# First conditioning of a hybrid decoder step: the rests all on VectorE, eight weight slots whole in fp32, the first norm's tiles made between the groups, the constants loaded in two parts

## The chip, the cores and the metric

The kernel runs on one core of one Trainium2 chip. The metric is the device time of one execution in microseconds, the median of several runs. The engines are TensorE (PE in the profile), VectorE (DVE), ScalarE (ACT), GpSimd (POOL) and SyncE (SP), which issues most of the transfers.

## What is computed

One step of a single-layer hybrid decoder, for a prompt of 256 tokens and a sample group of 8 sequences with 4 tokens each: 288 token columns in all. D_MODEL is 2048. The part that matters here is the start of the layer:

```python
ada = jnp.dot(jax.nn.silu(c), p["w_ada"]) + p["b_ada"]
sh1, sc1, gt1, sh2, sc2, gt2 = jnp.split(ada[:, None, :], 6, axis=-1)
h = _rmsnorm(x, p["g_norm1"]) * (1.0 + sc1) + sh1
(qkv_raw, z, a_raw, b_raw, dq, dk, dv, iq, ik, iw, gate_gdn, gate_dsa) = _split_cols(jnp.dot(h, p["w_in"]))
```

c has nine rows (one for the prompt, eight for the samples). Behind it come gated DeltaNet, sparse attention, their merge, a convolutional feed-forward part and a last norm; the other four parts of ada are made later in the kernel, among other work. All is fp32 outside.

## The kernel before

**Split products.** A product of fp32 accuracy is made of cheaper ones. A weight slot is a tile of 128 x (4 x 256) fp32, 512 KB. ScalarE rounds it into w_hi (function hi, L703, type fp32r); VectorE or GpSimd subtracts, rest = raw - w_hi (L1199 and L648), into the place where the raw values are; TensorE multiplies with both. For the conditioning (cond_slot, L1988 and L1992) the activations cact (silu(c), high part and rest, 20 columns) are the stationary side: four products of 256 columns with w_hi and four with rest. For w_in (slot, L2022, L2023 and L2027) the weights are stationary and h_hi and h_lo, 288 columns, run through: 16 products with w_hi, 8 with rest.

**First conditioning ("ada1").** 16 groups of four slots: group g makes 256 columns of shift1 (g < 8) or scale1 (g >= 8). A group sums into one bank; VectorE copies it (cond_copy, L1184) to cond_t, TensorE turns it with two small products against the constant fold (turn, L2010) and VectorE adds the bias (cond_bias, L1190) into ada. The even slots' rests are GpSimd's, the odd ones' VectorE's. In each group TensorE also multiplies one tile of squares of x by ones (norm_part, L2055), behind one ScalarE square (squares_of, L716). These loops are rolled, two groups per pass.

**First norm.** When all groups are done: rms on ScalarE (Ln and Exp, L722 and L724), then scale_shift on VectorE: amul = (1 + scale) * g (L1219), the samples' tile hs in three operations (L1224 to L1228), and for each of 16 tiles of x a product into hf (L1231); ScalarE adds the shift and rounds (h_round, L729 to L734), GpSimd makes h_lo (h_rest, L653), VectorE that of the samples (L1234). w_in's first product waits for hs_lo and for the h_lo of the first four tiles.

**Order.** Each engine runs its own list in the order written. SyncE loads the slots in order (L563, L568); a load waits for raw_free of its ring place, which TensorE gives when the slot is used. Rings: 8 raw tiles and 4 w_hi tiles in the conditioning, 6 and 3 in w_in. c, all constants, vec, heads_v and x are loaded from ScalarE's queue at the start. ScalarE's list has the square between the third and the fourth hi of each group; before the first it waits for x.

## Time and profile before

| | us |
|---|---|
| median of 3 runs (lowest, highest) | 2187.02 (2181.03, 2190.06) |
| profiled execution, whole | 2179.57 |
| its span in the profile | 2177.6 |
| TensorE busy | 2043.4 (94%) |
| VectorE, ScalarE, GpSimd busy | 802.3, 1024.2, 1458.8 |
| mean granted TensorE clock | 0.979 |

All times within the execution count from the span's start. "Busy" is the time in which an engine executes; the rest is waiting. The conditioning and the first norm take the first 148 us of the span.

### The profile page before, as it was taken

The numbers are of one execution on the slowest core, as the hardware profiler recorded it, in microseconds if no ns is written. First come the engines' busy times: TensorE is split into PE (matmuls) and PEld (weight loads), VectorE is DVE, ScalarE is ACT, GpSimd is POOL, SyncE is SP. The second block draws the span as 40 slices with busy tenths as digits, with TensorE's granted clock in tenths as the row PEclk, the third lists the DMA queues.
The fourth block names the chain that finished last, engine by engine and source line by source line (L and its number), as shares of the span: only waits on it lengthen the run. The fifth ranks groups of instructions, "written<-read, shape, count | busy, mean of one in ns | idle before, by whom it ended". The sixth has DMA issues, their size and how long they took to land.

```text
span 2177.6 us, 39902 instructions
## 1 busy us (share of the span) xinstructions
PE 2043.4 (94%) x15252; PEld 1953.2 (90%) x15252; DVE 802.3 (37%) x1833; ACT 1024.2 (47%) x1580; POOL 1458.8 (67%) x625
## 2 busy tenths in 40 slices
PE   5769999999899998999989969999999999999996
PEld 3559989999898897988989969999999999999996
DVE  4654644443534446354534122232112232113212
ACT  5564335664445445455453336555334444344432
POOL 5777555674665565656678658777777777777762
PEclk9989999999999999999999989999999999999998
DMA  9856533443566575565676434444454444455541
GB/s 341 287 169 205 174 116 132 146 158 126 178 213 210 198 244 194 201 227 199 238 220 216 140 113 143 167 164 164 165 166 168 167 164 164 164 166 169 167 166 68
DMA packets 128418, 390.76 MB, mean 179 GB/s; under 512 B 27490, under 2 KB 36002, under 8 KB 127778
## 3 DMA queue, kind: packets, MB, share of 16 engines
q1 hardware_dynamic: 107008, 365.74, 49.6%
q10 hardware_dynamic: 21282, 23.25, 3.3%
q8 instruction: 88, 1.44, 0.3%
q14 instruction: 40, 0.33, 0.1%
HBM read 379.99 MB, written 8.88 MB: 179 GB/s over the span
## 4 chain that ended last, share of the span: by engine, by line
PE 85%; DVE 5%; ACT 3%; issue 2%; POOL 2%; DMA 2%; DVEq 1%; ACTq 0%
PE bank L2022 23%; PE bank L2023 23%; PE bank L2027 23%; PE bank L1992 3%; PE bank L1988 2%; POOL rest_a L648 1%; DVE rest_a L1199 1%; PE bank L2369 1%; PE bank L2361 1%; DVE rest_b L1199 1%; PE bank L2372 1%; PE bank L2055 1%; DMA x<-in_x 1%; PE bank L2465 1%; PE bank L2292 1%
## 5 line engine op out<-in xcount | busy, mean ns | idle before, releaser
L648 POOL TENSOR_TENSOR rest_a<-raw_a,hi_a 128x1024 fp32r<-128x1024 f32 x217 | 536.4, 2477 | 267.3 <-ACT hi_a L703 266.9
L2022 PE MATMUL bank<-h_hi,hi_a 128*128 128x288 f32 x1592 | 439.9, 302 | 18.3 <-POOL h_lo L653 13.2
L2023 PE MATMUL bank<-h_lo,hi_a 128*128 128x288 f32 x1592 | 432.8, 297 | 0.0
L703 ACT ACTIVATE hi_a<-raw_a 128x1024 fp32r<-128x1024 f32 x257 | 270.7, 1058 | 339.3 <-PE bank L2027 267.0
L648 POOL TENSOR_TENSOR rest_a<-raw_a,hi_b 128x1024 fp32r<-128x1024 f32 x100 | 241.6, 2416 | 130.6 <-ACT hi_b L703 130.6
L2022 PEld LDWEIGHTS bank<-h_hi,hi_a 128*128 128x128 f32 x1592 | 303.0, 190 | 22.1 <-issue 19.6
L2023 PEld LDWEIGHTS bank<-h_lo,hi_a 128*128 128x128 f32 x1592 | 303.6, 191 | 0.4
L648 POOL TENSOR_TENSOR rest_b<-raw_b,hi_a 128x1024 fp32r<-128x1024 f32 x82 | 205.1, 2501 | 85.8 <-ACT hi_a L703 85.8
L2027 PE MATMUL bank<-h_hi,rest_a 128*128 128x288 f32 x1656 | 252.7, 295 | 0.5
L2027 PEld LDWEIGHTS bank<-h_hi,rest_a 128*128 128x128 f32 x1656 | 230.5, 188 | 1.9 <-POOL rest_a L648 1.9
L2022 PE MATMUL bank<-h_hi,hi_b 128*128 128x288 f32 x776 | 213.5, 301 | 0.5 <-ACT hi_b L703 0.5
L2023 PE MATMUL bank<-h_lo,hi_b 128*128 128x288 f32 x776 | 210.0, 296 | 0.0
L703 ACT ACTIVATE hi_b<-raw_a 128x1024 fp32r<-128x1024 f32 x119 | 125.9, 1058 | 144.1 <-PE bank L2027 110.8
L703 ACT ACTIVATE hi_a<-raw_b 128x1024 fp32r<-128x1024 f32 x98 | 103.7, 1058 | 140.1 <-PE bank L2027 109.7
L2022 PEld LDWEIGHTS bank<-h_hi,hi_b 128*128 128x128 f32 x776 | 146.8, 189 | 2.2 <-ACT hi_b L703 0.7
L2023 PEld LDWEIGHTS bank<-h_lo,hi_b 128*128 128x128 f32 x776 | 147.2, 190 | 0.3
L1863 DVE SCALAR_TENSOR_TENSOR x<-bank,ada,x 128x256 f32<-128x256 f32 x64 | 28.0, 479 | 321.0 <-PE bank L2027 321.0
L648 POOL TENSOR_TENSOR rest_c<-raw_c,hi_b 128x1024 fp32r<-128x1024 f32 x47 | 112.9, 2403 | 39.7 <-ACT hi_b L703 39.7
L648 POOL TENSOR_TENSOR rest_a<-raw_a,hi_c 128x1024 fp32r<-128x1024 f32 x39 | 93.8, 2405 | 56.1 <-ACT hi_c L703 56.1
L648 POOL TENSOR_TENSOR rest_b<-raw_b,hi_c 128x1024 fp32r<-128x1024 f32 x39 | 93.7, 2402 | 34.8 <-ACT hi_c L703 34.8
L648 POOL TENSOR_TENSOR rest_c<-raw_c,hi_a 128x1024 fp32r<-128x1024 f32 x39 | 94.0, 2409 | 31.3 <-ACT hi_a L703 31.3
L2022 PE MATMUL bank<-h_hi,hi_c 128*128 128x288 f32 x352 | 95.9, 298 | 17.0 <-ACT hf L734 17.0
(475 smaller groups left out, 4452.7 us busy)
## 6 DMA issues: line engine op xcount, KB each, us to landing
raw_a<-in_stream SPq DMA_DIRECT2D x423, 512.0 KB, 3.4
raw_b<-in_stream SPq DMA_DIRECT2D x167, 512.0 KB, 3.3
raw_c<-in_stream SPq DMA_DIRECT2D x94, 512.0 KB, 3.3
st<-in_state ACTq DMA_DIRECT2D x16, 512.0 KB, 5.4
out_state_s<-st ACTq DMA_DIRECT2D x8, 512.0 KB, 4.8
x<-in_x ACTq DMA_DIRECT2D x1, 2304.0 KB, 17.1
x<-in_x ACTq DMA_DIRECT2D x2, 1152.0 KB, 6.1
...
```

The lines of the kernel that those rows point to most:

```text
L648: nc.gpsimd.tensor_tensor(rest[r], raw[r], w_hi[q].bitcast(f32), ALU.subtract).then_inc(lo_ready, 1)
L703: A_(w_hi[q], raw[r], ACT.Copy).then_inc(hi_ready, 1)
L1199: T_(rest[r], raw[r], w_hi[q].bitcast(f32), ALU.subtract).then_inc(lo_dve, 1)
L1863: STT(xt[:, 0:SEQ], bank[2 * bs + c][:, 0:SEQ], gt[:, 0:1], xt[:, 0:SEQ], ALU.mult, ALU.add)
L1988: MM(out[0:2 * NCP, 0:CT * P], cact[:, s_ * KS + k, :, :].rearrange("p m n -> p (m n)"), w_hi[q][:, k, :], start=(s_ == 0 and k == 0), sto ...
L1992: last = MM(out[0:NCP, 0:CT * P], cact[:, s_ * KS + k, 0, :], rest[r][:, k, :], start=False, stop=(s_ * KS + k == KT - 1))
L2022: MM(banks[c][:, 0:N], w_, hi_of(k), start=(first and k == 0), stop=False)
L2023: ins = MM(banks[c][:, 0:N], w_, lo_of(k), start=False, stop=False)
L2027: ins = MM(banks[c][:, 0:N], rest[r][:, k, c * P:(c + 1) * P], hi_of(k), start=False, stop=(last_ and k == KS - 1))
L2055: MM(bank[7][:, 0:N], ones, sq[:, s_ % 2, :], start=(s_ == 0), stop=(s_ == KT - 1)).then_inc(sq_used, 1)
L2292: last = MM(bank[7][:, TURN_COL + c * NCP:TURN_COL + (c + 1) * NCP], cond_t[:, c * P:(c + 1) * P], cv["fold"][0:2 * NCP, :], start=True, s ...
L2361: ins = MM(blk(3, ch), bt[:, l % 2, ch, :], tt[:, 4 + ch, :], start=True, stop=True)
```

## The change

- **Order of the groups.** ADA_GROUP: shift and scale groups by turns, so that after each pair two tiles of h can be made. All loops of the stage are written out.
- **Rests.** All 56 rests of split slots are VectorE's (ada_rest). GpSimd has none in this stage; its list goes on with w_in's.
- **Whole slots.** Slots 1 and 3 of groups 8 to 11 are multiplied in plain fp32 (whole_slot: the unsplit c_f, ten columns, against the raw tile): no hi, no rest.
- **Squares.** Four ScalarE squares of four tiles each (square_quad, groups 2 to 5) into sq1; the 16 products with ones in groups 3 to 6, one behind each slot; rms behind group 7's hi.
- **x scaled in place.** VectorE multiplies x by the norm's factor, four tiles at a time (scale_x, groups 8 to 11). ScalarE makes h_hi and hf of two tiles from it (round_pair, from group 9 on), VectorE h_lo (lo_pair), and the samples' part four tiles at a time (samples, round_samples, lo_samples).
- **The end.** The last turn stands behind w_in's slot 0, the last pair is made while w_in runs.
- **Loads.** The constants are reordered; the first 268 columns are loaded at the start, the other part by SyncE behind w_in's sixth load; w_in's slot 1 waits for it. x is loaded from ScalarE's queue behind the third hi.

```diff
+WHOLE = [4 * n + s for n in range(8, 12) for s in (1, 3)]
+SPLIT_BEFORE = [j - sum(1 for w in WHOLE if w < j) for j in range(2 * KT // CT * (KT // KS) + 1)]
+NSPLIT = SPLIT_BEFORE[-1]
+SUM_AT, SQUARE_AT, RMS_AT, XR_AT, PAIR_AT = 3, 2, 7, 8, 9
+SAMPLE_AT = {9: 0, 10: 1, 13: 2}
+def ada_slot(j):
+    return 4 * ADA_GROUP[j // 4] + j % 4
 def in_slot(j):
...
+CONST_SIZE = {"ident": P, "ones": P, "fold": NCP, "eps": 1, "one": 1, "neg": P, "lev": LV * P, "neg_s": P, "lev_s": 2 * P, "pnm": NS, "maskb": DB * NS,
               "bcol": DB, "rope": 4 * N, "rotm": 2 * P, "causal": 2 * SEQ, "causal_s": L_S,
-              "sel": H, "tsel": NS, "fold": NCP, "eps": 1, "one": 1}
+              "sel": H, "tsel": NS}
+CONST_1 = 2 * P + NCP + 2
...
         qkv = pl.take("qkv", [P, QKV_T, N])
...
-            if BASE["in"] <= s_ < BASE["go"]:
-                return (s_ - BASE["in"]) % RING_I, s_ + i * per
-            return (s_ + (RING - 1 if s_ >= BASE["go"] else 0)) % RING, s_ + i * per
-        assert BASE["in"] % RING == 0 and BASE["go"] % RING == 0 and (BASE["go"] - BASE["in"]) % RING_I == 2
+            cnt = s_ - len(WHOLE) + i * per
+            if s_ < BASE["go"]:
+                return (s_ - BASE["in"]) % RING_I, cnt
+            return (s_ + RING - 1) % RING, cnt
...
+                if n == 0:
+                    for j in range(BASE["in"]):
+                        r, use = raw_at("ada1", j)
+                        load_one(r, use, ada_slot(j))
+                    continue
                 if n == 1:
                     for j in range(4 * N_IN):
                         r, use = raw_at("in", j)
                         load_one(r, use, in_slot(j))
+                        if j == RAW_I - 1:
+                            sp.dma_start(consts[:, CONST_1:], A["consts"][:, CONST_1:]).then_inc(const_in, 16)
...
-            with pool.Fori(0, LO_DVE // 4) as i:
-                for j in range(0, 8, 2):
-                    lo("ada1", j, i, 8)
-            for j in range(RING_I):
-                lo("in", j)
-            h_rest(0)
-            for j in range(RING_I, 4 * N_IN):
+            for j in range(4 * N_IN):
...
-            act.dma_start(consts[:, :], A["consts"]).then_inc(const_in, 16)
+            act.dma_start(consts[:, 0:CONST_1], A["consts"][:, 0:CONST_1]).then_inc(const_in, 16)
             act.dma_start(vec[:, :], A["vec"]).then_inc(const_in, 16)
             act.dma_start(heads_v[:, :], A["heads_v"]).then_inc(const_in, 16)
-            act.dma_start(x[:, :, :].rearrange("p k n -> p (k n)"), A["x"]).then_inc(x_in, 16)
...
+            def square_quad(q):
+                act.wait_ge(x_in, 16)
+                A_(sq1[:, 4 * q:4 * q + 4, :], x[:, 4 * q:4 * q + 4, :], ACT.Square).then_inc(sq_ready, 1)
+            def round_pair(m):
+                act.wait_ge(h_t, m + 1)
+                act.wait_ge(xr_ready, m // 2 + 1)
+                act.wait_ge(h_lo_ready, 2 * m + 2)
+                for k in (2 * m, 2 * m + 1):
+                    A_(h_hi[:, k, 0:SEQ], x[:, k, 0:SEQ], ACT.Identity, scale=amul[:, k, 0:1], bias=ada[:, k, 0:1])
+                    last = A_(hf[:, k % HB, :], x[:, k, 0:SEQ], ACT.Identity, scale=amul[:, k, 0:1], bias=ada[:, k, 0:1])
+                last.then_inc(h_hi_ready, 2)
+            def round_samples(b):
+                act.wait_ge(hs_t, b + 1)
+                A_(h_hi[:, 4 * b:4 * b + 4, SEQ:], hs[:, 4 * b:4 * b + 4, :], ACT.Copy).then_inc(hs_hi, 1)
...
-            with act.Fori(0, KT // 2) as i:
-                for s_ in range(2):
-                    for j in range(3):
-                        hi("ada1", 4 * s_ + j, i, 8)
-                    act.wait_ge(x_in, 16)
-                    squares_of(0, i, s_)
-                    hi("ada1", 4 * s_ + 3, i, 8)
-            act.wait_ge(const_in, 48)
-            rms(0)
+            for n in range(2 * KT // CT):
+                for s_ in range(4):
+                    if 4 * n + s_ not in WHOLE:
+                        hi("ada1", 4 * n + s_)
+                    if (n, s_) == (0, 2):
+                        act.dma_start(x[:, :, :].rearrange("p k n -> p (k n)"), A["x"]).then_inc(x_in, 16)
+                    if s_ == 1 and SQUARE_AT <= n < SQUARE_AT + 4:
+                        square_quad(n - SQUARE_AT)
+                if n == RMS_AT:
+                    act.wait_ge(const_in, 48)
+                    rms(0)
+                if PAIR_AT <= n:
+                    round_pair(n - PAIR_AT)
+                if n - 1 in SAMPLE_AT:
+                    round_samples(SAMPLE_AT[n - 1])
             for j in range(RING_I):
                 hi("in", j)
-            h_round(0)
+            round_pair(KT // CT - 1)
+            round_samples(3)
...
+                q, n = split_at("ada1", j)
+                dve.wait_ge(hi_ready, n + 1)
+                T_(rest[r], raw[r], w_hi[q].bitcast(f32), ALU.subtract).then_inc(lo_dve, 1)
+            def cond_copy(n):
+                wait_group(dve, "ada1", n)
+                CP(cond_t[:, :], bank[2 * (n % 2)][0:2 * NCP, 0:CT * P]).then_inc(cond_cp, 1)
+            def cond_bias(n):
+                t = CT * ADA_GROUP[n]
+                dve.wait_ge(cond_done, n + 1)
+                T_(ada[:, t:t + CT, :], bank[2 * (n % 2) + 1][:, 0:CT * NCP].rearrange("p (c n) -> p c n", c=CT)[:, :, 0:NC],
+                   vec[:, V_BADA + t:V_BADA + t + CT].unsqueeze(2).to_broadcast([P, CT, NC]), ALU.add).then_inc(grp_free[n % 2], 1)
+                if n % 2:
+                    dve.drain()
+                    k = t - KT
+                    STT(amul[:, k:k + CT, :], ada[:, t:t + CT, :], 1.0, vec[:, V_G1 + k:V_G1 + k + CT].unsqueeze(2).to_broadcast([P, CT, NC]),
+                        ALU.add, ALU.mult).then_inc(h_t, 1)
+            def scale_x(q):
+                xq = x[:, 4 * q:4 * q + 4, :]
+                T_(xq, xq, bank[7][:, 0:N].unsqueeze(1).to_broadcast([P, 4, N]), ALU.mult).then_inc(xr_ready, 1)
+            def lo_pair(m):
+                k = 2 * m
+                dve.wait_ge(h_hi_ready, k + 2)
+                T_(h_lo[:, k:k + 2, 0:SEQ], hf[:, k % HB:k % HB + 2, :], h_hi[:, k:k + 2, 0:SEQ].bitcast(f32),
+                   ALU.subtract).then_inc(h_lo_ready, 2)
+            tb4 = lambda a: a.rearrange("p k (t b) -> p k t b", b=DB)
+            of_b = lambda a: a.unsqueeze(2).to_broadcast([P, 4, TS, DB])
+            def samples(b):
+                k = slice(4 * b, 4 * b + 4)
+                dve.drain()
+                T_(tb4(hs[:, k, :]), tb4(x[:, k, SEQ:]), of_b(amul[:, k, 1:NC]), ALU.mult)
+                dve.drain()
+                T_(tb4(hs[:, k, :]), tb4(hs[:, k, :]), of_b(ada[:, k, 1:NC]), ALU.add).then_inc(hs_t, 1)
+            def lo_samples(b):
+                k = slice(4 * b, 4 * b + 4)
+                dve.wait_ge(hs_hi, b + 1)
+                T_(h_lo[:, k, SEQ:], hs[:, k, :], h_hi[:, k, SEQ:].bitcast(f32), ALU.subtract).then_inc(hs_lo, 1)
             dve.sem_inc(cond_cp, 2)
-            ada1_pair(0)
-            with dve.Fori(0, KT // CT - 2) as i:
-                ada1_pair(2, i)
-            ada1_pair(KT - 2)
-            cond_bias(KT - 1)
-            dve.wait_ge(x_in, 16)
+            for n in range(2 * KT // CT):
+                for s_ in range(4):
+                    if 4 * n + s_ not in WHOLE:
+                        ada_rest(4 * n + s_)
+                    if s_ == 0 and n >= 2:
+                        if n == 2:
+                            dve.wait_ge(const_in, 48)
+                        cond_bias(n - 2)
+                    if s_ == 1 and n >= 1:
+                        cond_copy(n - 1)
+                    if s_ == 2 and n > PAIR_AT:
+                        lo_pair(n - PAIR_AT - 1)
+                    if s_ == 2 and n - 2 in SAMPLE_AT:
+                        lo_samples(SAMPLE_AT[n - 2])
+                    if s_ == 3 and XR_AT <= n < XR_AT + 4:
+                        if n == XR_AT:
+                            dve.wait_ge(rs_ready, 1)
+                        scale_x(n - XR_AT)
+                if n in SAMPLE_AT:
+                    samples(SAMPLE_AT[n])
+            cond_bias(2 * KT // CT - 2)
+            cond_copy(2 * KT // CT - 1)
+            lo_pair(KT // CT - 2)
+            cond_bias(2 * KT // CT - 1)
+            samples(3)
+            lo_pair(KT // CT - 1)
+            lo_samples(3)
             dve.drain()
...
-            scale_shift(0, 0)
-            dve.drain()
...
+                    pe.wait_ge(lo_dve, cnt + 1)
+                elif name == "mix" and ON_DVE[j]:
+                    pe.wait_ge(lo_dve, NSPLIT + LO_BEFORE[j] + 1)
+                elif name == "mix":
+                    pe.wait_ge(lo_ready, BASE["mix"] - BASE["in"] + LO_BEFORE[j] + 1)
                 else:
-                    pe.wait_ge(lo_dve, i * (per // 2) + (j // 2 + 1))
+                    pe.wait_ge(lo_ready, cnt + (1 - NSPLIT - (0 if name == "in" else NDVE)))
             def cond_slot(name, out, j, s_, i=0, per=0):
...
+                    last = MM(bank[2 * (n % 2)][0:NCP, 0:CT * P], c_f[:, s_ * KS + k, :], raw[r][:, k, :],
+                              start=False, stop=(s_ * KS + k == KT - 1))
+                last.then_inc(raw_free[r], 1)
+            def cond(n, s_):
                 if s_ == 0:
-                    pe.wait_ge(cond_cp, i * per + (g + 1))
-                cond_slot("ada1", bank[2 * (g % 2)], 4 * g + s_, s_, i, 4 * per)
-            def turn(g, i=0, per=0):
-                bs, cnt = grp("ada1", 2, g, i, per)
-                pe.wait_ge(cond_cp, i * per + (g + 3))
+                    pe.wait_ge(cond_cp, n + 1)
+                cond_slot("ada1", bank[2 * (n % 2)], 4 * n + s_, s_)
...
+                    last.then_inc(ssq_ready, 1)
             pe.wait_ge(c_ready, 2)
-            def ada1_pair(first, i=0):
-                for g in (first, first + 1):
-                    for s_ in range(KT // KS):
-                        cond(g, s_, i, 2)
-                        if s_ == 1:
-                            if g > 0:
-                                turn(g - 1, i, 2)
-                            if g == 0:
-                                pe.wait_ge(const_in, 48)
-                            norm_part(0, g, i)
-                            if g == KT - 1 and first == KT - 2:
-                                norm_end(0)
-            ada1_pair(0)
-            with pe.Fori(0, KT // CT - 2) as i:
-                ada1_pair(2, i)
-            ada1_pair(KT - 2)
-            turn(KT - 1)
+            for n in range(2 * KT // CT):
+                for s_ in range(KT // KS):
+                    if 4 * n + s_ in WHOLE:
+                        whole_slot(n, s_)
+                    else:
+                        cond(n, s_)
+                    if s_ == 2 and n >= 1:
+                        if n == 1:
+                            pe.wait_ge(const_in, 48)
+                        turn(n - 1)
+                    if SUM_AT <= n < SUM_AT + 4:
+                        first_sum(4 * (n - SUM_AT) + s_)
             def rotate(n):
...
-                        pe.wait_ge(hs_lo, 1)
                     if n == 0:
+                        pe.wait_ge(hs_lo, s_ + 1)
                         pe.wait_ge(h_lo_ready, HB + (s_ + 1) * KS)
                         pe.wait_ge(h_hi_ready, (s_ + 1) * KS)
+                    if (n, s_) == (0, 1):
+                        turn(2 * KT // CT - 1)
+                        pe.wait_ge(const_in, 64)
```

## Rows read from the trace of the kernel before

**Rows 1.** Busy time by stretches: busy us (instructions), granted clock, transfers' share, GB/s

```profile
core 0: us, PE busy (x) PEld busy (x) DVE busy (x) ACT busy (x) POOL busy (x), PEclk, DMA share, GB/s
100.00:120.00 20.00, 15.05 (x108) 10.39 (x109) 13.50 (x13) 11.70 (x14) 15.67 (x7) 1.00 0.87 287
150.00:160.00 10.00, 10.00 (x70) 10.00 (x70) 3.06 (x7) 9.77 (x21) 9.23 (x11) 0.90 0.34 112
```

**Rows 2.** The chain that ended last, in order of time: start us, us, what

```profile
112.75 2.77 DVE rest_b L1199
...
116.21 0.55 PE bank L2010 x4
117.03 1.80 DVE rest_c L1199
...
119.89 2.78 DVE rest_a L1199
...
133.23 0.46 PE bank L1988 x4
```

**Rows 3.** One of the rests' four forms on VectorE: ns lowest, median, highest

```profile
L1199 DVE TENSOR_TENSOR rest_a<-raw_a,hi_a x8: 1226/2722/2773, 12.7 to 119.9; 128x1024 fp32r<-128x1024 f32 x8
```

**Rows 4.** Instructions in order of time, four rests and a follower: start us, us, engine

```profile
112.03 2.39 POOL L648 TENSOR_TENSOR rest_c<-raw_c,hi_b 128x1024 fp32r<-128x1024 f32 x1 [1.44 <-ACT hi_b L703]
114.37 3.37 POOL L648 TENSOR_TENSOR rest_a<-raw_a,hi_a 128x1024 fp32r<-128x1024 f32 x1
582.62 1.22 DVE L1629 TENSOR_TENSOR rest_b<-raw_b,hi_a 128x1024 fp32r<-128x1024 f32 x1
583.75 0.69 DVE L1681 TENSOR_TENSOR bt<-bank,consts 128x512 f32<-128x512 f32 x1
```

**Rows 5.** The same view, in the first 25 us

```profile
12.67 1.23 DVE L1199 TENSOR_TENSOR rest_a<-raw_a,hi_a 128x1024 fp32r<-128x1024 f32 x1 [12.67 <-ACT hi_a L703]
20.42 0.44 ACT L716 ACTIVATE sq<-x 128x288 f32 x1 [5.78 <-DMA x<-in_x]
```

**Rows 6.** Busy time by short stretches, the columns of rows 1

```profile
20.00:22.00 2.00, 0.99 (x3) 0.66 (x3) 0.16 (x1) 1.58 (x3) 0.00 (x0) 1.00 1.03 410
68.00:70.00 2.00, 2.00 (x11) 1.36 (x10) 0.47 (x2) 1.63 (x3) 1.68 (x1) 0.50 0.55 152
150.00:152.00 2.00, 2.00 (x10) 2.00 (x10) 1.14 (x3) 2.00 (x7) 1.88 (x3) 0.50 0.00 0
```

**Rows 7.** Instructions in order of time, 132 to 154 us

```profile
132.17 1.28 ACT L722 ACT_TABLE_LOAD   x1 [3.92 <-PEq L2059]
134.19 0.41 DVE L1184 COPY cond_t<-bank 20x256 f32<-20x256 f32 x1 [1.54 <-PE bank L1992]
135.59 1.99 ACT L703 ACTIVATE hi_a<-raw_a 128x1024 fp32r<-128x1024 f32 x2
136.74 2.89 DVE L1226 TENSOR_TENSOR hs<-hs,amul 128x512 f32<-128x512 f32 x1
148.43 0.58 PE L2022 MATMUL bank<-h_hi,hi_a 128*128 128x288 f32 x1 [13.16 <-POOL h_lo L653]
153.29 0.30 PE L2022 MATMUL bank<-h_hi,hi_a 128*128 128x288 f32 x1
```

**Rows 8.** TensorE's matmuls in order of time, behind 183 us

```profile
183.23 1.13 PE L2089 MATMUL bank<-rt,consts 128*128 128x288 f32 x4
...
184.34 0.29 PE L2023 MATMUL bank<-h_lo,hi_a 128*128 128x288 f32 x1
184.47 0.29 PE L2022 MATMUL bank<-h_hi,hi_a 128*128 128x288 f32 x1
```

**Rows 9.** Transfers by line: count, size of one, us from issue to landing

```profile
raw_a<-in_stream SPq DMA_DIRECT2D x423, 512.0 KB, 3.4
...
x<-in_x ACTq DMA_DIRECT2D x1, 2304.0 KB, 17.1
```

**Rows 10.** The samples' tile hs, both norms: ns lowest, median, highest

```profile
L1226 DVE TENSOR_TENSOR hs<-hs,amul x2: 693/1790/2886, 136.7 to 1295.6; 128x512 f32<-128x512 f32 x2
```

More of the change, by code:

```diff
@@ L78 @@
 UNITS = KV + QH
+ADA_GROUP = [n // 2 + (n % 2) * (KT // CT) for n in range(2 * KT // CT)]
+WHOLE = [4 * n + s for n in range(8, 12) for s in (1, 3)]
[5 more added lines that the diff above has]
+    return 4 * ADA_GROUP[j // 4] + j % 4
 def in_slot(j):
@@ L305, in decoder_step @@
         og = Place(qkv_at).take("og", [P, 2 * H, N], f32r)
+        sq1 = Place(qkv_at).take("sq1", [P, KT, N])
         qkv = pl.take("qkv", [P, QKV_T, N])
@@ L1179, in _ @@
             row = lambda a: a.rearrange("p k n -> p (k n)")
-            def cond_copy(g, i=0, per=0):
-                wait_group(dve, "ada1", g, i, per)
-                CP(cond_t[:, :], bank[2 * (g % 2)][0:2 * NCP, 0:CT * P]).then_inc(cond_cp, 1)
-            def cond_bias(g, i=0, per=0):
-                dve.wait_ge(cond_done, i * per + (g + 1))
-                t = i * (per * CT) + g * CT
-                T_(ada[:, ds(t, CT), :], bank[2 * (g % 2) + 1][:, 0:CT * NCP].rearrange("p (c n) -> p c n", c=CT)[:, :, 0:NC],
-                   vec[:, ds(t + V_BADA, CT)].unsqueeze(2).to_broadcast([P, CT, NC]), ALU.add).then_inc(grp_free[g % 2], 1)
@@ L1193, in ada1_pair @@
-            def ada1_pair(first, i=0):
-                for g in (first, first + 1):
-                    for j in (4 * g + 1, 4 * g + 3):
-                        r, _ = raw_at("ada1", j, i, 8)
-                        q, n = split_at("ada1", j, i, 8)
-                        dve.wait_ge(hi_ready, n + 1)
-                        T_(rest[r], raw[r], w_hi[q].bitcast(f32), ALU.subtract).then_inc(lo_dve, 1)
-                        if j % 4 == 1 and g > 0:
-                            cond_bias(g - 1, i, 2)
-                    cond_copy(g, i, 2)
-                    if g == 0:
-                        dve.wait_ge(const_in, 48)
@@ L1520, in last_tables @@
                 dve.drain()
+            dve.wait_ge(const_in, 64)
             cos_part(0)
@@ L1969, in wait_rest @@
                 _, cnt = split_at(name, j, i, per)
[L1970 to L1978 removed]
+                if name == "ada1":
+                    pe.wait_ge(lo_dve, cnt + 1)
[3 more added lines that the diff above has]
+                    pe.wait_ge(lo_ready, BASE["mix"] - BASE["in"] + LO_BEFORE[j] + 1)
                 else:
[L1980 removed]
+                    pe.wait_ge(lo_ready, cnt + (1 - NSPLIT - (0 if name == "in" else NDVE)))
             def cond_slot(name, out, j, s_, i=0, per=0):
@@ L1996, in cond_slot, with whole_slot, turn @@
                 last.then_inc(raw_free[r], 1)
-            def cond(g, s_, i=0, per=0):
-                if s_ == 0:
-                    pe.wait_ge(cond_cp, i * per + (g + 1))
-                cond_slot("ada1", bank[2 * (g % 2)], 4 * g + s_, s_, i, 4 * per)
-            def turn(g, i=0, per=0):
-                bs, cnt = grp("ada1", 2, g, i, per)
-                pe.wait_ge(cond_cp, i * per + (g + 3))
+            def whole_slot(n, s_):
+                r, use = raw_at("ada1", 4 * n + s_)
+                pe.wait_ge(raw_in[r], use * 16 + 16)
+                for k in range(KS):
+                    last = MM(bank[2 * (n % 2)][0:NCP, 0:CT * P], c_f[:, s_ * KS + k, :], raw[r][:, k, :],
+                              start=False, stop=(s_ * KS + k == KT - 1))
+                last.then_inc(raw_free[r], 1)
+            def cond(n, s_):
+                if s_ == 0:
+                    pe.wait_ge(cond_cp, n + 1)
+                cond_slot("ada1", bank[2 * (n % 2)], 4 * n + s_, s_)
+            def turn(n):
+                bs, cnt = grp("ada1", 2, n)
+                pe.wait_ge(cond_cp, n + 3)
                 pe.wait_ge(grp_free[bs], cnt + 1)
@@ L2051, in _, with norm_part, first_sum @@
             hh, hl = (lambda k: h_hi[:, k, :]), (lambda k: h_lo[:, k, :])
[L2053 to L2054 removed]
+            def norm_part(n, s_):
+                pe.wait_ge(sq_ready, 4 + (n - 1) * KT + s_ + 1)
                 MM(bank[7][:, 0:N], ones, sq[:, s_ % 2, :], start=(s_ == 0), stop=(s_ == KT - 1)).then_inc(sq_used, 1)
             def norm_end(n):
[L2058 removed]
+                pe.wait_ge(sq_used, n * KT + 2)
                 pe.sem_inc(ssq_ready, 1)
[L2061 to L2080 removed]
+            def first_sum(k):
+                pe.wait_ge(sq_ready, k // 4 + 1)
+                last = MM(bank[7][:, 0:N], ones, sq1[:, k, :], start=(k == 0), stop=(k == KT - 1))
+                if k == KT - 1:
+                    last.then_inc(ssq_ready, 1)
+            pe.wait_ge(c_ready, 2)
+            for n in range(2 * KT // CT):
[10 more added lines that the diff above has]
+                        first_sum(4 * (n - SUM_AT) + s_)
             def rotate(n):
```

36 lines of the change are left out of this document (12 added, 24 removed).

## The prediction

> **What bounds the kernel now.** I read the page first: TensorE is busy 94% of a 2177.6 us span, so only a stage in which it waits can give anything. The busy time by stretches [rows 1] finds two such stages. In the first conditioning (0 to 134 us) TensorE is busy 15 to 16 us of every 20, of which one stands there. Between 134 and 148 us it does nothing, and from 150 us on it is busy all the time. The reader is to see that VectorE, ScalarE and GpSimd each have 12 to 16 us of work in 20 us and none is full: it is a chain, not one engine.
>
> The chain of waits [rows 2] shows one steady group: VectorE rest, TensorE, VectorE rest, TensorE, and so on. From the start of one long rest (112.75) to that of the next group (119.89) it is 7.14 us, and 4.6 of them are two VectorE rests, of 2.77 and 1.80 us. The same subtraction takes 1.226 us at its fastest and 2.7 us at its median on the tiles of raw_a [rows 3]. What differs is who else runs: at 12.67 GpSimd is idle, at 112.75 it is in a subtraction of its own that ends at 114.42, and VectorE's ends 1.10 us after that; GpSimd's next (114.37) takes 3.37 us, not 2.39, and holds up VectorE's at 117.03 in turn [rows 4, 5]. So the two engines take turns, and the rests on the path cost about twice their own time. The Trainium skill's page "SBUF — State Buffer", section "SBUF: two separate sides", says that a VectorE operation with two SBUF inputs and a GpSimd operation that reads SBUF exclude each other for the whole instruction. By that rule too a rest with GpSimd idle takes its own 1.23 us, so the sum would be the same.
>
> The head [rows 5]: ScalarE's square sits ahead of the fourth hi and waits until 20.42 for x, which takes 17.1 us to land [rows 5, 9]. Everything stands still from 15 to 20.4 us. The transfers don't: 408 to 414 GB/s in each 2 us from 20 to 30, of which one stands there [rows 6], and later, with the eight slots full, they fall back to some 290 GB/s [rows 1], which is what the consumers take.
>
> The tail [rows 7]: the last copy at 134.19, then in a row turn, bias, amul, three operations on hs (the second alone 2.89), the h_lo of the samples and the prompt's tiles of h, up to the first product of w_in at 148.43. TensorE's granted clock is 0.50 (the 1.2 GHz level) in all stretches from 142 to 152 us after this idling, of which the last stands there [rows 6]; the first slot of w_in takes 148.43 to 153.29, 4.86 us, where a later one takes 24 x 0.132 = 3.17 us [rows 7, 8].
>
> **The change, part by part.** The stage is then a pipeline with several near-equal limits per group of four slots, so I price each and take the largest, stretch by stretch.
>
> *All rests on VectorE, GpSimd out.* A rest alone starts 1.13 us before the next instruction (582.62 to 583.75) [rows 4]. A group costs VectorE 4 x 1.13 + copy 0.41 + bias 0.10 to 0.18 = 5.1 us. Upper bound: 2.0 us a rest, halfway between alone and overlapped, if something else than GpSimd slows it; nothing in the rows does, since the one at 12.67 ran while the queues moved over 400 GB/s.
>
> *Transfers.* 64 slots of 512 KB are 33.55 MB, x 2.36, vec 0.30, c 0.08 [rows 9], the first 268 columns of the constants 0.14: 36.4 MB. At the 411 GB/s that rows 6 show, 88.6 us from about 2.5 us on, 5.1 us a group (four slots, 2.10 MB). This is the floor: the last slot lands at 91, and hi, rest and product add 3.2: 94. The Trainium skill's "HBM Reference", section "Specifications (TRN2)", gives 358 GB/s as each core's share when both cores of a pair stream and some 425 for one that streams alone; the floor would be 107 by the one and 91 by the other. The trace stands by the second, with 408 to 414 GB/s.
>
> *TensorE, at the clock of 1.00.* Four hi products take 0.46 us in the chain [rows 2], four of rest as long; back to back I count 0.88 for a split slot. A turn is 0.55 [rows 2]. A slot whole in fp32 is four products of 256 columns. No row shows it; the nearest is two fp32 products of 288 columns between 183.23 and the stream's resuming: the second product of the stream starts at 184.34, and one product's pitch of 0.13 is taken off that: 0.98 us for the two, 0.49 each [rows 8]. By columns 0.43 each, 1.7 a slot. Lower bound: a split slot's 0.88; upper: 4 x 0.49 = 2.0. I take 1.7, as the columns differ only by 256 to 288. The sums of squares cost 0.49 each as before, but now sit four to a group in groups 3 to 6. So a group is 3.5 + 0.55 = 4.1 us; groups 3 to 6 are 4.1 + 1.9 = 6.0; groups 8 to 11 are 2 x 0.88 + 2 x 1.7 + 0.55 = 5.7.
>
> *ScalarE.* hi is 1.0 us apart (two in 1.99) [rows 7]; groups 2 to 5 add one square of 1152 elements (0.44 us for 288 [rows 5]; about 1.2 for four times as many, since hi's 1024 take 1.0): 5.2 us. rms goes from 132.17 to 135.59, 3.4 us [rows 7], and now stands in group 7: ScalarE needs 7.4 us there. Its lead over TensorE (four hi slots) hides part; I take 6.5 us for the group, bounds 5.1 and 7.4. From group 9 on it has four activations of 128x256, at most 0.44 each as 288 columns take [rows 5], 1.7 us a group, beside two slots and later four: 5.7 us at most.
>
> *VectorE's moved tiles.* scale_x: 1152 elements a time, from 0.69 for 512 and 1.22 for 1024 [rows 4] about 1.35; lo_pair (512 elements, alone) 0.69; by the same two rows an operation of 128 elements or less is 0.3: samples 0.8 with its drains, lo_samples 0.3, amul 0.3. In groups 8 to 11 there are only two rests (2.3), so the sum stays at 4.2 to 5.6, under TensorE's 5.7. In groups 12 to 15: 5.1 + 0.69, plus 0.3, 1.1, 0, 0.6: 25.2 us for the four. Here VectorE is the bound. The product on hs took 2.89 us at 136.74 beside GpSimd, and 0.693 at its other place [rows 7, 10].
>
> *x's load behind the third hi.* It shares the queue's rate with slots 3 to 9: 9.2 MB by slot 11 is 2.5 + 22.4 us, plus 3.2 us to work it off: the first three groups end at 28. The wait for x moves to group 2, where x has about landed; 0 to 2 us, taken as nothing because those transfers are counted in the 28.
>
> Sum: 28 + 4 x 6.0 + 6.5 + 4 x 5.7 + 25.2 = 106.5, less two rests that VectorE has in hand when its own stretch begins (2.3): the last conditioning product at **104** us, against 134.2: 30 us.
>
> *The tail.* h is ready for slot 0 before the conditioning ends. In ScalarE's order round_pair(6) stands ahead of hi of w_in's slot 0; it ends about with the conditioning, GpSimd's rest is 2.4 to 3.4 us behind, while TensorE has 2.1 us of hi products: slot 0 takes 4.4 us. Then the last turn, 0.55, and the wait for the constants' second part. That is 2.0 MB, issued behind the load of w_in's slot 5, for which conditioning slot 61 must be done (about 3 us before the end): behind 0.5 MB and at 411 GB/s it lands some 5 us after the end. Wait 0 to 1; bound 6, if the queue still has four slots ahead of it. So slot 1 starts at the end + 6, and did at + 19.1 (153.29 - 134.16): 13 us. Slot 3 needs the last pair: turn at + 5, bias and amul, 1.7 us ScalarE, the samples and the pair beside GpSimd 2 to 3 us: ready at + 10, wanted at + 12. Hidden, by 2 us only. GpSimd then starts w_in's rests with nothing in hand (2.4 to 3.4 us a slot against 3.17), where before it had three; a wait of up to 1 us in the first slots.
>
> Together 30 + 13 = 43 us. The profiled execution is 2179.57 us, its span 2177.6; it becomes 2136. It lies 7 us under the median of 2187.02, from which the forecast is **2144**. Everything behind 153 us is TensorE's stream, so it shifts as a whole. A change of this kernel can be told from none from about 0.5% (11 us) on.
>
> **The rivals.**
> *Rests stay slow, the head and tail alone give.* If a rest takes 2.0 us in VectorE's bare order (not GpSimd but the fourfold load of one engine), the 56 rests add 49 us to 63, less what other limits cover: the end is at about 128, gain 6 + 13: 2168. For it: no long run of rests on VectorE alone is in the trace. Against: 1.23 at 12.67 and 1.22 at 582.62 [rows 4, 5]. Chance 8%.
> *The limits don't overlap.* Each group waits in turn for ScalarE, VectorE and TensorE, because only four hi tiles and no second cond_t stand between them; 1 us more in each of 16 groups, and the constants' second part 4 us late: 2144 + 20 = 2164. For it: today's group is such a chain. Against: a slot's way (1.06 + 1.23 + 0.45 = 2.7 us) is shorter than four slots (5.1). Chance 12%.
> *The transfers alone set the end.* The stretches smooth each other out and the end comes at 94 to 97: 2135. Chance 14%.
> *Slower: TensorE at the 1.2 GHz level.* The granted clock fell to 0.50 at 68 us, and in two more such spells (82, 126), while this stage ran at three quarters busy [rows 6]. TensorE's work is 56 x 0.88 + 8 x 1.7 + 16 x 0.55 + 16 x 0.49 = 80 us at the upper level and 160 at the lower: the end at 167, slot 1 at 173, 20 us later than before: 2207. It decides from the point where the end passes 147 us, about 86 us at the lower level. Against: each spell lasted under 4 us, and now TensorE has less idle time in a group, not more. Chance 3%.
>
> **How the numbers follow.** The forecast's own case (63%) is 2138 to 2154: stretches moved by their bounds. The range 2131 to 2161 takes in the transfer case and most of the chained one; outside are the slow rests, the low clock and the end of the chained case, under 2 in 10. Faster by over 0.5% (under 2176) 0.95, within 0.02, slower 0.03.
>
> **What would show it.** The last conditioning product near 104; rests of 1.23 us throughout; whole slots of 1.7 us; groups 8 to 11 with TensorE full and 12 to 15 with VectorE full; first w_in product under 2 us after; GpSimd's first rest only then. Wrong: rests near 2 us, ScalarE idle on transfers in groups 3 to 15, a TensorE wait of over 3 us behind the last turn.

## The result, and the profile after

| | us |
|---|---|
| before, median of 4 runs | 2185.16 (2181.03 to 2190.06) |
| changed kernel, median of 4 runs | 2152.01 (2148.54 to 2154.36) |
| ratio, 95% interval | 0.9855, 0.9823 to 0.9886 |
| profiled execution, its span | 2154.01, 2152.2 |

The kernel became 33 us faster; the forecast was 43 (2144), the range 2131 to 2161. In the two profiles the last conditioning product ends at 109.2 us against 134.2, and w_in's slot 1 at 123.1 against 156.6: 33.5 us. These two ends are the marks by which all runs are compared below, since each is read in one trace to 0.1 us, while whole runs of one kernel spread by 5 to 18 us. Each mark comes from one trace of its kernel.

In this kernel's trace L2076 and L2080 are a split slot's products with w_hi and with rest, L2091 is a whole slot, L2161 a sum of squares, L2107 a turn; L2119, L2120 and L2124 are w_in's products (h_hi and h_lo with w_hi, h_hi with rest).

Busy time by stretches, changed kernel (the columns of [rows 1]):

```profile
20.00:30.00 10.00, 9.78 (x54) 6.64 (x55) 9.23 (x12) 9.26 (x10) 0.00 (x0) 0.64 1.03 409
40.00:50.00 10.00, 10.00 (x71) 7.36 (x69) 8.40 (x12) 7.84 (x8) 0.00 (x0) 1.00 0.93 316
80.00:90.00 10.00, 10.00 (x67) 5.76 (x65) 9.11 (x14) 8.29 (x13) 0.00 (x0) 1.00 0.93 331
100.00:110.00 10.00, 8.66 (x64) 5.72 (x63) 9.27 (x15) 9.31 (x13) 2.61 (x1) 1.00 0.98 373
...
119.00:121.00 2.00, 2.00 (x10) 2.00 (x9) 0.00 (x0) 0.00 (x0) 1.08 (x1) 0.50 0.00 0
```

TensorE, busy 15 us of 20 before [rows 1], is full from 30 to 60 and from 70 to 90 us (in between it waits 1.15 us behind ScalarE's rms). Behind 90 us VectorE sets the pace: all of TensorE's waits there are for VectorE's rests (one stands below, at 98.11). ScalarE is as busy (9.31 against 9.27), but it runs ahead: it rounds the last slot at 103.34, and VectorE gets to that slot's rest at 107.29. The same kernel's groups by form (busy us, mean ns, idle before):

```profile
L1230 DVE TENSOR_TENSOR rest_a<-raw_a,hi_a 128x1024 fp32r<-128x1024 f32 x16 | 19.4, 1215 | 9.6 <-ACT hi_a L720 9.6
L1230 DVE TENSOR_TENSOR rest_c<-raw_c,hi_c 128x1024 fp32r<-128x1024 f32 x8 | 9.7, 1208 | 0.1
L1252 DVE TENSOR_TENSOR x<-x,bank 128x1152 f32<-128x1152 f32 x4 | 5.3, 1334 | 0.0
```

A rest takes 1.21 us on average, where the median of this form was 2.7 [rows 3]. The instructions in order of time, at the head and in the last groups and the tail:

```profile
7.88 0.36 ACTq L779 DMA_DIRECT2D x<-in_x  x1
18.85 1.06 ACT L720 ACTIVATE hi_b<-raw_c 128x1024 fp32r<-128x1024 f32 x1 [5.03 <-DMA raw_c<-in_stream]
...
98.11 0.64 PE L2080 MATMUL bank<-rest_a,cact 128*10 128x256 f32 x4 [0.78 <-DVE rest_a L1230]
...
106.19 0.42 SPq L617 DMA_DIRECT2D consts<-in_consts  x1
109.02 0.29 PE L2119 MATMUL bank<-h_hi,hi_a 128*128 128x288 f32 x1
112.28 0.61 PE L2107 MATMUL bank<-consts,cond_t 20*128 20x10 f32 x4
117.04 0.61 PE L2119 MATMUL bank<-h_hi,hi_a 128*128 128x288 f32 x1 [4.15 <-DMA consts<-in_consts]
121.05 2.04 PE L2124 MATMUL bank<-h_hi,rest_a 128*128 128x288 f32 x8
```

ScalarE waits 5.03 us for slot 6's tile, whose transfer is under way together with x's. The first product of w_in starts with the end of the conditioning, where the kernel before has TensorE idle for 13.16 us [rows 7]. But slot 1 then waits 4.15 us for the constants' second part, which lands 10.8 us after its issue. Behind the wait the granted clock is 0.50 (the 1.2 GHz level): slot 1 ends 6.05 us after 117.04, 2.9 us more than 24 x 0.132.

The chain, in order of time, gives TensorE's prices in the middle:

```profile
78.21 0.54 PE bank L2107 x4
78.75 1.82 PE bank L2091 x8
80.58 0.57 PE bank L2076 x4
81.15 0.46 PE bank L2080 x4
81.61 1.82 PE bank L2091 x8
83.44 0.57 PE bank L2076 x4
84.01 0.46 PE bank L2080 x4
84.47 0.54 PE bank L2107 x4
```

From turn to turn, 78.21 to 84.47, a group with two whole slots takes 6.26 us: 2 x 1.82 (whole slots; x8, because each of the four fp32 products leaves two records), 2 x 1.03 (split slots, each behind a whole one) and 0.54 (turn). Groups 3 to 6 show 6.39 in the same way.

The two profiled executions differ by 25.6 us and not by 33.5. At the second norm (its amul, 1290.8 before and 1263.0 after) 5.7 of the missing 8 us are already gone, and the rest by the end. Both traces have spells at the lower clock level up to there, most of them at matching places; the changed kernel's has some where the other has none. One of them is at 800 us; first its busy time, then that of the kernel before at the matching place:

```profile
800.00:802.00 2.00, 2.00 (x11) 1.92 (x10) 1.02 (x4) 1.01 (x1) 2.00 (x2) 0.50 0.33 117
```

```profile
830.00:834.00 4.00, 4.00 (x33) 3.92 (x31) 2.99 (x8) 1.06 (x1) 4.00 (x2) 1.00 0.86 316
```

The medians (33.2 us apart) agree with the stage, and the profile before lies 5.6 us under its kernel's median, so I take the 8 us for the luck of one profile. From the end of slot 1 to the end of the span the twelve traces of this document take 2017.8 to 2029.9 us, 2021.0 in the kernel before and 2029.1 in the changed one. The two lowest belong to kernels with the old order (e5 and before), so whether the change makes such spells more frequent is not settled.

### The profile page after: what moved, and what is told of

It reads as the page before. It is cut to its first block, busy times and chain, and to the rows that moved or that the text cites. A ratio compares the mean times of both kernels' runs of the same rounds, so it can differ in the third digit from the quotient of the medians.

```text
span 2152.2 us, 39472 instructions
## 1 busy us (share of the span) xinstructions
PE 2052.0 (95%) x15252; PEld 1957.8 (91%) x15252; DVE 808.6 (38%) x1868; ACT 1017.8 (47%) x1563; POOL 1356.9 (63%) x577
## 4 chain that ended last, share of the span: by engine, by line
PE 88%; DVE 3%; ACT 3%; issue 2%; DMA 2%; POOL 1%; DVEq 1%; ACTq 0%; SPq 0%; POOLq 0%
PE bank L2119 24%; PE bank L2120 23%; PE bank L2124 23%; PE bank L2080 3%; PE bank L2076 3%; PE bank L2469 1%; PE bank L2461 1%; POOL rest_a L672 1%; PE bank L2472 1%; PE bank L2565 1%; PE bank L2392 1%; DMA raw_c<-in_stream 1%; PE bank L2091 1%; PE bank L2544 1%; PE bank L2152 1%
## 5 line engine op out<-in xcount | busy, mean ns | idle before, releaser
L672 POOL TENSOR_TENSOR rest_a<-raw_a,hi_a 128x1024 fp32r<-128x1024 f32 x209 | 509.1, 2440 | 364.9 <-ACT hi_a L720 364.8
L2119 PE MATMUL bank<-h_hi,hi_a 128*128 128x288 f32 x1592 | 441.4, 303 | 8.6 <-DMA consts<-in_consts 4.1
L2120 PE MATMUL bank<-h_lo,hi_a 128*128 128x288 f32 x1592 | 434.2, 298 | 0.0
L2119 PEld LDWEIGHTS bank<-h_hi,hi_a 128*128 128x128 f32 x1592 | 304.1, 191 | 13.0 <-issue 6.0
L2120 PEld LDWEIGHTS bank<-h_lo,hi_a 128*128 128x128 f32 x1592 | 304.8, 191 | 0.4
L672 POOL TENSOR_TENSOR rest_a<-raw_a,hi_b 128x1024 fp32r<-128x1024 f32 x92 | 223.9, 2434 | 119.0 <-ACT hi_b L720 119.0
L2124 PE MATMUL bank<-h_hi,rest_a 128*128 128x288 f32 x1656 | 254.8, 296 | 0.3
L2124 PEld LDWEIGHTS bank<-h_hi,rest_a 128*128 128x128 f32 x1656 | 233.0, 190 | 1.5 <-POOL rest_a L672 1.5
L672 POOL TENSOR_TENSOR rest_b<-raw_b,hi_a 128x1024 fp32r<-128x1024 f32 x74 | 179.2, 2422 | 86.1 <-ACT hi_a L720 86.1
L2119 PE MATMUL bank<-h_hi,hi_b 128*128 128x288 f32 x776 | 213.5, 301 | 0.0
L2120 PE MATMUL bank<-h_lo,hi_b 128*128 128x288 f32 x776 | 210.0, 296 | 0.0
L720 ACT ACTIVATE hi_a<-raw_b 128x1024 fp32r<-128x1024 f32 x94 | 99.2, 1058 | 137.3 <-PE bank L2124 112.8
L2119 PEld LDWEIGHTS bank<-h_hi,hi_b 128*128 128x128 f32 x776 | 146.9, 189 | 1.5 <-ACT hi_a L720 0.3
L2120 PEld LDWEIGHTS bank<-h_lo,hi_b 128*128 128x128 f32 x776 | 147.2, 190 | 0.3
L2119 PE MATMUL bank<-h_hi,hi_c 128*128 128x288 f32 x352 | 96.1, 299 | 17.0 <-ACT hf L771 17.0
L672 POOL TENSOR_TENSOR rest_c<-raw_c,hi_b 128x1024 fp32r<-128x1024 f32 x39 | 93.6, 2401 | 28.7 <-ACT hi_b L720 28.7
```

Of the source, the lines that this page charges most:

```text
L672: nc.gpsimd.tensor_tensor(rest[r], raw[r], w_hi[q].bitcast(f32), ALU.subtract).then_inc(lo_ready, 1)
L720: A_(w_hi[q], raw[r], ACT.Copy).then_inc(hi_ready, 1)
L2119: MM(banks[c][:, 0:N], w_, hi_of(k), start=(first and k == 0), stop=False)
L2120: ins = MM(banks[c][:, 0:N], w_, lo_of(k), start=False, stop=False)
L2124: ins = MM(banks[c][:, 0:N], rest[r][:, k, c * P:(c + 1) * P], hi_of(k), start=False, stop=(last_ and k == KS - 1))
```

## The experiments

"Last product" is the end of the last conditioning product, "slot 1" that of w_in's slot 1.

| run | last product | slot 1 | whole, us |
|---|---|---|---|
| before | 134.2 | 156.6 | 2185.16 |
| changed kernel | 109.2 | 123.1 | 2152.01 |
| e5: before, all rests on VectorE | 135.1 | 157.2 | 2176.82 (one run) |
| e8: before, order alone | 124.0 | 146.1 | 2172.74 (one run) |
| e9: both | 102.0 | 124.6 | 2152.41 (one run) |
| e3: changed, half the rests on GpSimd | 118.1 | 133.3 | 2164.53 (one run) |
| e4: changed, no slot whole | 114.9 | 128.5 | 2152.46 (one run) |
| e1: changed, constants earlier | 111.0 | 118.0 | 2142.56 (4 runs) |
| e6: e1, tiles behind | 108.9 | 125.7 | 2155.47 (one run) |
| e7: e1, twelve slots whole | 110.7 | 117.8 | 2144.70 (one run) |
| e11: e1, x in four parts | 109.0 | 116.1 | 2147.74 (one run) |
| e10: all three | 107.9 | 115.0 | 2139.07 (4 runs) |

**Where the conditioning's 25 us come from: e5, e8, e9, e3.** e5 edits the kernel before:

```diff
-            with pool.Fori(0, LO_DVE // 4) as i:
-                for j in range(0, 8, 2):
-                    lo("ada1", j, i, 8)
...
-                    for j in (4 * g + 1, 4 * g + 3):
+                    for j in range(4 * g, 4 * g + 4):
```

> The kernel before with one edit: all 64 rests on VectorE, GpSimd has none in the conditioning. Theory A, the turns of the two engines set the pitch: a group takes 5.3 to 5.8 us in place of 7.15, the last conditioning product comes near 106 to 110 in place of 134.2, the first norm behind it still takes 14 us, and w_in starts at 120 to 124 in place of 148.4. Theory B, one engine with the rests in series is no better than two: a group stays at 6.8 to 7.2 us and w_in starts at 143 or later.

Theory A fell: 135.1. Each rest takes its own time now, and yet a group takes 7.3 us. In order of time (here L1987 is products with rest, L2005 the turn):

```profile
102.25 0.61 PE L2005 MATMUL bank<-consts,cond_t 20*128 20x10 f32 x4
103.04 0.18 DVE L1187 TENSOR_TENSOR ada<-bank,vec 128x18 f32 x1 [1.41 <-PE bank L2005]
103.15 1.23 DVE L1196 TENSOR_TENSOR rest_c<-raw_c,hi_b 128x1024 fp32r<-128x1024 f32 x1
104.30 1.22 DVE L1196 TENSOR_TENSOR rest_c<-raw_c,hi_c 128x1024 fp32r<-128x1024 f32 x1
104.43 0.63 PE L1987 MATMUL bank<-rest_c,cact 128*10 128x256 f32 x4 [0.42 <-DVE rest_c L1196]
106.24 0.41 DVE L1181 COPY cond_t<-bank 20x256 f32<-20x256 f32 x1 [0.72 <-PE bank L1987]
106.62 2.36 DVE L1196 TENSOR_TENSOR rest_a<-raw_a,hi_a 128x1024 fp32r<-128x1024 f32 x2
107.90 0.64 PE L1987 MATMUL bank<-rest_a,cact 128*10 128x256 f32 x4 [1.13 <-DVE rest_a L1196]
```

VectorE's list has the copy right behind the group's last rest and the bias right behind the second rest of the next: at each it stands (0.72 and 1.41 us) until TensorE is through, and TensorE then stands for the next rest. That led to theory C, and to e8, in which rests are shared as before and only copy, bias and turn stand later. e9 has e5's edit too, and its BIAS_AT is 0, the first of the four rests:

```diff
+        BIAS_AT = 1
...
+                        if j % 4 == BIAS_AT and g > 1:
+                            cond_bias(g - 2, i, 2)
                         if j % 4 == 1 and g > 0:
-                            cond_bias(g - 1, i, 2)
-                    cond_copy(g, i, 2)
+                            cond_copy(g - 1, i, 2)
...
+                        if s_ == 2 and g > 0:
+                            turn(g - 1, i, 2)
                         if s_ == 1:
-                            if g > 0:
-                                turn(g - 1, i, 2)
```

> The kernel before, rests shared by both engines as before, with the order alone changed: VectorE copies a group's bank one rest (two slots) later, behind the next group's first rest, adds the bias a group later, and TensorE turns behind the third slot and not the second. Theory C, formed after the kernel before with all rests on VectorE still took 7.3 us a group although each rest took 1.22: VectorE's copy right behind the group's own last rest makes it wait for TensorE and TensorE for the next rest, so the place of the copy sets the pitch and the last conditioning product comes at 118 to 128 in place of 134.2. Theory A, the turns of the two engines alone set it: it stays at 132 or later.

> The same order with all 64 rests on VectorE: both edits together, nothing else of the change. Theory C, the two edits are worth much together and the second nothing alone: VectorE needs 4 x 1.13 + 0.5 = 5.1 us a group and its last product comes at 100 to 106; the first norm then takes its 14 us and w_in starts at 114 to 120. Rival, something else of the change (written-out loops, x loaded later, squares by fours) carries the gain: the last product stays beyond 115.

124.0 and 102.0: as theory C had it. e5's edit alone gives -0.9 us (a loss), e8's 10.2, both together 32.2. Two limits lay at nearly the same height. With the order mended and two engines at work, the turns are the limit; e8 in order of time:

```profile
101.73 3.37 POOL L649 TENSOR_TENSOR rest_b<-raw_b,hi_a 128x1024 fp32r<-128x1024 f32 x1
102.78 3.41 DVE L1200 TENSOR_TENSOR rest_b<-raw_b,hi_a 128x1024 fp32r<-128x1024 f32 x1
105.07 3.36 POOL L649 TENSOR_TENSOR rest_c<-raw_c,hi_b 128x1024 fp32r<-128x1024 f32 x1
106.53 2.98 DVE L1200 TENSOR_TENSOR rest_c<-raw_c,hi_c 128x1024 fp32r<-128x1024 f32 x1
```

Both are nearly always in a rest. Each ends about 1.1 us (VectorE) or 2.25 us (GpSimd) after the other: a pair takes 3.35 us, a group 6.7, where VectorE alone needs 5.1. The Trainium skill's page "SBUF — State Buffer", section "SBUF: two separate sides", calls this an exclusive lock, which whichever operation starts first holds for its whole instruction. The trace agrees: VectorE's rest of 102.78 ends 1.09 us behind GpSimd's of 101.73. In e9 the next limit is reached:

```profile
40.00:50.00 10.00, 9.67 (x76) 6.89 (x74) 9.38 (x11) 8.85 (x11) 0.00 (x0) 1.00 1.03 411
80.00:90.00 10.00, 9.84 (x76) 6.93 (x75) 9.97 (x13) 8.70 (x11) 0.00 (x0) 1.00 1.03 410
```

The queues move 410 GB/s without a pause, and VectorE is full as well (9.97): both need 5.1 us a group.

e3 gives the even rests of the changed kernel back to GpSimd.

```diff
+            for j in range(0, BASE["in"], 2):
+                lo("ada1", j)
...
-                    if 4 * n + s_ not in WHOLE:
+                    if s_ % 2 and 4 * n + s_ not in WHOLE:
                         ada_rest(4 * n + s_)
```

> The changed kernel with the rests of slots 0 and 2 of each group on GpSimd again, all else as changed. Theory A, the two engines taking turns was the cost: rests go back to 1.7 to 2.8 us on VectorE, a group with two VectorE and two GpSimd rests to some 7 us, and as 12 groups have it and the other four have GpSimd alone, the last conditioning product comes at 120 to 132 instead of 109. Theory B, the written-out order, the moved norm and the head gave the gain and not the rests: it stays at 105 to 112.

118.1, between the two: the engines' turns cost 8.9 us in the new order too (rests of raw_c on VectorE 2.50 us on average, on GpSimd 3.27). That is less than A's bound because other limits cover most of it: groups 3 to 6 take 6.7 us where TensorE's own work needed 6.39, and groups 8 to 11 take 6.26 in both kernels. By the turn in group 12 (93.48 us against 89.64) 3.8 of the 8.9 us are there. The rest comes in the last groups, where one wait is followed by a granted clock of 0.50 from 106 to 114 us:

```profile
103.42 0.64 PE L2084 MATMUL bank<-rest_c,cact 128*10 128x256 f32 x4 [2.11 <-DVE rest_c L1232]
```

**The whole slots: e4, e7.**

```diff
-WHOLE = [4 * n + s for n in range(8, 12) for s in (1, 3)]
+WHOLE = []
```

> No slot whole in fp32, all 64 split. Theory A, whole slots relieve VectorE, which would be the bound of groups 8 to 11 with four rests (4.5), copy and bias (0.5), x (1.3) and more (0.5 to 1): 7 us a group against 5.7, so the last conditioning product is 4 to 6 us later, at 113 to 115. Theory B, the fp32 products cost TensorE 0.9 us a slot more than they save on VectorE: the last product is at 107 to 109.

114.9, 5.7 us later, as theory A had it; a group of 8 to 11 takes 6.97 us from turn to turn (72.94, 79.91) against 6.26, with VectorE at 9.83 us of 10 and TensorE at 7.55 (72 to 82 us). The whole time (2152.46, one run) doesn't show this: the marks do. e7 adds to WHOLE slot 1 of groups 12 to 15, beside e1's edit:

> The constants' second part behind slot 40 as well, and four more slots whole in fp32, slot 1 of each of groups 12 to 15. Theory A, VectorE is the bound there: 1.13 us less a group on it, until TensorE (4.9) or the transfers (5.1) bind: the last product comes 3 to 4.5 us earlier than 111.0 and slot 1 ends near 114. Theory B, with 2 MB more to move the transfers bind there: it moves by under 1.5 us.

Theory B by its number, 110.7 against 111.0, but not by its reason. Busy time of e7:

```profile
90.00:100.00 10.00, 10.00 (x69) 6.14 (x67) 9.21 (x17) 8.24 (x12) 0.00 (x0) 1.00 0.95 351
100.00:110.00 10.00, 9.83 (x65) 5.58 (x63) 7.95 (x13) 9.89 (x15) 0.73 (x1) 1.00 1.01 401
```

In e1 the same two stretches have TensorE at 8.45 and 8.76 and VectorE at 9.74 and 9.91. VectorE got air, and TensorE, with a slot of 1.82 us more in each group, became the limit at 5.38 us from turn to turn (92.55 to 97.93), with the transfers (5.1) just under it.

**The tail: e1, e6.**

```diff
                         load_one(r, use, ada_slot(j))
+                        if j == 40:
+                            sp.dma_start(consts[:, CONST_1:], A["consts"][:, CONST_1:]).then_inc(const_in, 16)
...
-                        if j == RAW_I - 1:
-                            sp.dma_start(consts[:, CONST_1:], A["consts"][:, CONST_1:]).then_inc(const_in, 16)
```

> The constants' second part is loaded behind the conditioning's slot 40 and not behind w_in's sixth slot. Theory A, the load alone was late: TensorE's wait of 4.1 us ahead of w_in's slot 1 goes and with it the 1.2 GHz level in that slot (6.0 us against 3.2), so slot 1 ends near 116 and not at 123.1, 7 us gained, while the conditioning's last product stays within 1 us of 109.0, since its end is VectorE's. Theory B, the transfers are the bound throughout (share 0.93 to 1.0): the 2 MB push the conditioning's end by their 5 us to 114, and slot 1 ends at 121 to 123, 0 to 2 us gained.

Between the theories, nearer A: the last product 1.8 us later, slot 1 5.1 us earlier, and slot 1 runs at the upper level (112.92 to 116.83 from rests to rests with a turn between). The ratio to before is 0.9803 (0.9780 to 0.9826) by four runs, 2142.56 us. That is 9.4 us under the changed kernel, of which the mark explains 5.1; where the rest comes from no run shows.

```profile
112.92 1.22 PE L2124 MATMUL bank<-h_hi,rest_a 128*128 128x288 f32 x8
114.07 0.61 PE L2107 MATMUL bank<-consts,cond_t 20*128 20x10 f32 x4
116.83 1.21 PE L2124 MATMUL bank<-h_hi,rest_a 128*128 128x288 f32 x8
```

e6, built on e1, takes round_pair, round_samples, lo_pair, samples and lo_samples out of the loop and puts them, in blocks of four tiles, behind it:

```diff
-                if PAIR_AT <= n:
-                    round_pair(n - PAIR_AT)
...
             for j in range(RING_I):
                 hi("in", j)
+            for b in range(3):
+                round_pair(2 * b)
+                round_pair(2 * b + 1)
+                round_samples(b)
+            round_pair(6)
...
```

> The changed kernel with the constants' second part loaded behind conditioning slot 40, and the norm's tiles (pairs and samples, not x's scaling) made behind the conditioning instead of between its groups. Theory A, the tiles are cheap between the groups and dear behind: groups 12 to 15 lose 0.7 us each of VectorE, so the last product comes 2 to 4 us earlier than 111.0, but w_in's first product waits 6 to 8 us for two pairs and the samples with GpSimd beside, and slot 1 ends 4 to 8 us later than 118.0. Rival, the two places cost the same: slot 1 ends within 2 us of 118.0.

Theory A: against e1 the last product is 2.0 us earlier and slot 1 7.7 us later. The first product waits 7.3 us, and the operation on hs takes 2.28 us beside GpSimd instead of 0.29:

```profile
PE bank L2119 <- DVE h_lo L1277: 7.3, 1, 7.3
```

**The head: e11, e10.** x in four parts, on e1:

```diff
-                    if (n, s_) == (0, 2):
-                        act.dma_start(x[:, :, :].rearrange("p k n -> p (k n)"), A["x"]).then_inc(x_in, 16)
+                    if (n, s_) in X_AT:
+                        k = 4 * X_AT.index((n, s_))
+                        act.dma_start(x[:, k:k + 4, :].rearrange("p k n -> p (k n)"), A["x"][:, k * N:(k + 4) * N]).then_inc(x_part[k // 4], 16)
```

> The changed kernel with the constants' second part behind slot 40, and x loaded in four parts from ScalarE's queue, behind the third hi of groups 0 to 3, each square waiting for its own part. Theory D, x's 2.36 MB in one piece is the hole of the head (ScalarE waits 5.0 to 5.7 us for slot 6's tile, TensorE then stays at the 1.2 GHz level until 28 us): the wait falls to 1 to 2 us, the level rises before 22 us, and the last conditioning product comes 2 to 4 us earlier than 111.0. Rival, the head is bound by the transfers whatever their order, and the bytes are the same: the last product moves by less than 1 us.

2.0 us earlier, the lower edge of theory D. ScalarE's wait falls from 5.7 us in one piece to 1.5 us in two, but the lower clock level doesn't go: e11 has a mean of 0.72 from 20 to 30 us and 0.94 in the next ten, e1 0.88, 0.61 and 1.00 from 10 to 40. The spell came later. In e1 it follows a wait of 4.9 us. In e11 TensorE has only short waits before it, none over 0.61 us, but is busy 2.4 us of the 4 from 20 to 24. Why the clock fell there stays open.

```profile
ACT hi_b L722 <- DMA raw_c<-in_stream: 1.5, 2, 1.1
```

> All three together: constants' second part behind slot 40, x in four parts, twelve slots whole. If the head's hole goes and the last groups are no longer VectorE's, the last product comes near 105 to 108 and slot 1 of w_in ends near 112 to 115, 38 us less than the kernel before by the median (ratio about 0.980 to 0.983); if the transfers hold the stage (38.4 MB at 409 GB/s from 2.5 us on, and 3.2 us of work behind the last, 99.6 us), nothing is gained on 110.7 but what the head gives.

107.9 and 115.0, both as expected, and slot 1 ends 41.7 us earlier than in the kernel before. Ratio 0.9814 (0.9769 to 0.9858), median 2139.07: by whole runs it can't be told from e1, and by slot 1 it is the best of these. e9's two small edits give by themselves about the whole time of the full change (2152.41, one run, against 2152.01): its conditioning ends 7.2 us earlier, and its norm behind it takes the gain back (slot 1 at 124.6 against 123.1).

## Why the prediction was right in kind, and where it was off

**The end of the conditioning, 104 forecast, 109.2 measured.** The method, the largest of several limits in each stretch, held; most terms were a little too small. Read off the chain, the stretches took: three groups 30.5 (28 forecast), groups 3 to 6 25.7 (24), group 7 some 5 (6.5), groups 8 to 11 25.6 (22.8), groups 12 to 15 22.3 (22.9). TensorE's prices were too low: 0.93 for a split slot (0.88) and 1.03 for one behind a whole slot, 1.82 for a whole one (1.7; the upper bound was 2.0), 0.48 and once in a group 0.68 for a sum (0.49). In the head, x's one piece of 2.36 MB was counted as bytes alone; it also made TensorE wait 4.2 us at slot 6, and behind that it ran at the 1.2 GHz level to about 27 us. e11, with x in four parts, has the end 2.0 us earlier.

**"All rests on VectorE": right price, wrong cause.** 1.21 us a rest throughout, as forecast. But the reading of the chain ("the two engines take turns, and the rests on the path cost about twice") stopped at one limit. e5 showed that without GpSimd's turns the old order takes 7.3 us a group. The sum escaped this because it assumed that in the new order all overlaps freely; that this held was in part luck. Copy, bias and turn stand later in the changed kernel. The diff shows it, but neither the list of the change nor the prediction names it as a part: the prediction prices copy and bias at their own 0.5 us. They were the half without which the other is worth nothing.

**The slow rests.** Refuted by each trace in which VectorE has the conditioning's rests alone (1.20 to 1.23 us). **Limits that don't overlap** (2164): the pipeline held, but its other half, the constants late, is what came. The prediction had "Wait 0 to 1; bound 6", with the condition that four slots are still ahead in the queue. The wait was 4.15 us, past the 3 us that the prediction named as a sign of being wrong; the part landed 7.8 us behind the end and not 5. This is the term that was sized wrong, and e1 shows it: with the load earlier the wait is gone. With it came a term that wasn't in the sum: behind this stall of 4 us TensorE came back at the lower level, which cost 2.9 us more. [Rows 6, 7] showed that pattern behind the old tail, and the sum used it only as a gain. The difference between forecast and measurement is 5.2 us at the end of the conditioning, 3.1 of waiting, 2.9 of clock, less 1.3 in slot 0 (3.1 us for a forecast 4.4): 9.9 us.

**The transfers as the only limit** (94 to 97): e9, which loads all constants first, comes near it: 102.0, where 38.4 MB at 409 GB/s and 5.7 us of start and work behind the last slot give 99.6. The changed kernel keeps 7 us off it, as TensorE's four sums a group and the whole slots exceed the 5.1 us of the transfers in groups 3 to 6 and 8 to 11.

**TensorE at the lower level throughout:** it didn't come; a spell from about 17 to 27 us (0.64 in the mean from 20 to 30) and the 0.50 behind the constants' wait are all that the stage had.

**The moved tiles** cost as priced (x's scaling 1.33 us, pairs 0.67 alone), and their place is worth 7.7 us by e6, of the 13 given for the tail. The whole slots pay where VectorE has the most to do (5.7 us in groups 8 to 11, e4) and hardly elsewhere (0.3 in groups 12 to 15, e7).
